# The last attention of a fused two-block transformer kernel: both scores of a query block for two heads issued back to back, then both masks

## What is computed

```python
def dsa_attention(q, k, v, iq, ik, iw, top_k):
    ...
        score = jnp.einsum('bqh,bqhk->bqk', iwb.astype(jnp.float32), jax.nn.relu(dots))
        score = jnp.where(admissible[None], score, -jnp.inf)
        _, sel = lax.top_k(score, top_k)
        kg = jax.vmap(lambda kb, ib: kb[ib])(k, sel)
        vg = jax.vmap(lambda vb, ib: vb[ib])(v, sel)
        valid = (sel // CHUNK) <= qchunk[None, :, None]
        s = jnp.einsum('bqhd,bqkd->bhqk', qb, kg, preferred_element_type=jnp.float32) * scale
        s = jnp.where(valid[:, None], s, -jnp.inf)
        p = jax.nn.softmax(s, axis=-1)
        return jnp.einsum('bhqk,bqkd->bqhd', p.astype(vg.dtype), vg)
```

## Time and profile before

| | |
|---|---|
| median of 3 runs | 2006.15 us (2005.57 to 2012.1) |
| the profiled execution | 2008.66 us, its span 2006.9 us |
| TensorE (PE) busy | 1967.6 us, 98% of the span |
| VectorE (DVE), ScalarE (ACT) busy | 51%, 36% |
| granted TensorE clock, mean | 0.991 of full |
| the last attention | from 1442.4 to about 1546 us |

### The profile page before, as it was taken

One profiled execution on the slowest core, in us unless ns is written; L12 is line 12 of the kernel. 1 busy time (PEld: TensorE's weight loads), 2 busy tenths in 40 slices (PEclk: granted clock), 3 DMA queues, 4 the chain that ended last, 5 costly groups with the idle time before them and its releaser, 6 DMA issues.

```text
span 2006.9 us, 25390 instructions
## 1 busy us (share of the span) xinstructions
PE 1967.6 (98%) x9146; PEld 1585.0 (79%) x9154; DVE 1014.1 (51%) x1572; ACT 719.8 (36%) x1214; POOL 79.1 (4%) x117
## 2 busy tenths in 40 slices
PE   9998999999999999999999999999999999999999
PEld 7776777877888888888888878767777878888887
DVE  6756335656565554633334345767734653333322
ACT  5455434432222222332223234345534433222221
POOL 0001000001111000000000010400000000000000
PEclk9998999999999999899999999999999999999999
DMA  5211122327666554333332323211111223333332
GB/s 173 82 56 63 53 64 73 95 94 231 207 215 210 178 173 147 100 94 94 96 97 89 116 73 95 75 53 43 43 43 43 84 74 116 94 94 103 96 105 94
DMA packets 57521, 207.20 MB, mean 103 GB/s; under 512 B 6449, under 2 KB 6577, under 8 KB 57441
## 3 DMA queue, kind: packets, MB, share of 16 engines
q1 hardware_dynamic: 46800, 167.68, 27.0%
q0 software_dynamic: 10640, 38.44, 6.2%
HBM read 203.96 MB, written 2.10 MB: 103 GB/s over the span
## 4 chain that ended last, share of the span: by engine, by line
PE 89%; DVE 5%; ACT 3%; issue 2%; DMA 1%; SPq 0%; DVEq 0%; ACTq 0%; POOLq 0%
PE PS L437 26%; PE PS L439 25%; PE PS L438 25%; PE PS L862 2%; PE PS L897 2%; PE PS L881 1%; PE PS L667 1%; DMA ADA<-ada 1%; ACT HI L1046 1%; PE PS L559 1%; DVE BIAS L1808 0%; PE PS L590 0%; DMA X<-x_in 0%; PE PS L641 0%; DVE SM L1807 0%
## 5 line engine op out<-in xcount | busy, mean ns | idle before, releaser
L437 PE MATMUL PS<-XH,HI 128*128 128x512 f32 x1552 | 628.9, 405 | 9.8 <-DVE GATE_1M L1876 3.5
L1450 DVE TENSOR_TENSOR LO<-RAW,HI 128x1024 fp32r<-128x1024 f32 x311 | 382.9, 1232 | 456.1 <-ACT HI L1046 455.2
L439 PE MATMUL PS<-XH,LO 128*128 128x512 f32 x1552 | 607.9, 392 | 0.0
L438 PE MATMUL PS<-XL,HI 128*128 128x512 f32 x1552 | 607.2, 391 | 0.0
L1046 ACT ACTIVATE HI<-RAW 128x1024 fp32r<-128x1024 f32 x311 | 328.7, 1058 | 591.9 <-PE PS L439 586.3
L437 PEld LDWEIGHTS PS<-XH,HI 128*128 128x128 f32 x1552 | 293.4, 189 | 88.7 <-issue 26.5
L439 PEld LDWEIGHTS PS<-XH,LO 128*128 128x128 f32 x1552 | 292.7, 189 | 63.1
L438 PEld LDWEIGHTS PS<-XL,HI 128*128 128x128 f32 x1552 | 293.8, 189 | 53.1 <-issue 0.2
L437 PE MATMUL PS<-HIDH,HI 128*128 128x512 f32 x528 | 205.5, 389 | 0.0
L439 PE MATMUL PS<-HIDH,LO 128*128 128x512 f32 x528 | 205.5, 389 | 0.0
L438 PE MATMUL PS<-HIDL,HI 128*128 128x512 f32 x528 | 205.4, 389 | 0.0
(11 more groups left out here) (345 smaller groups left out, 2072.7 us busy)
## 6 DMA issues: line engine op xcount, KB each, us to landing
RAW<-weights SPq DMA_DIRECT2D x311, 512.0 KB, 3.6
ADA<-ada POOLq DMA_DIRECT2D x72, 512.0 KB, 4.6
X<-x_in SPq DMA_DIRECT2D x4, 512.0 KB, 7.1
y_out<-X SPq DMA_DIRECT2D x8, 256.0 KB, 4.6
SQC<-squares SPq DMA_DIRECT2D x1, 320.0 KB, 9.2
TAB_P<-positions POOLq DMA_DIRECT2D x1, 256.0 KB, 4.7
POS<-positions POOLq DMA_DIRECT2D x1, 256.0 KB, 3.3
LAMS<-lambdas POOLq DMA_DIRECT2D x1, 128.0 KB, 5.4
```

Source lines behind the costliest of these rows:

```text
L437: mm(bank, a, moving[0][:, t, :], start=start, stop=False)
L438: mm(bank, a, moving[1][:, t, :], start=False, stop=False)
L439: ins = mm(bank, z, moving[0][:, t, :], start=False, stop=stop)
L1450: V.tensor_tensor(LO[n0 % 3][:], RAW[n0 % 3][:], HI[n0 % 3][:].bitcast(F32), ALU.subtract)\
```

## The change

For attention 3 the units are numbered by pairs of heads: `unit(3, u)` gives head `2 * (u // 8) + u % 2` and block `u % 8 // 2`. So units 0 and 1 are block 0 of heads 0 and 1, units 2 and 3 block 1 of the same heads, and so on. ScalarE and VectorE keep their steps and use the new numbering. TensorE issues scores in even steps alone: both scores, then both masks. The second score now waits, at step `u`, for `probs` of unit `u - 2`, where it waited at step `u + 1` for the same unit. Attentions 1 and 2 stay as they were.

```diff
+        def unit(a, u):
+
+            if a == 3:
+                return 2 * (u // 8) + u % 2, u % 8 // 2
+            return divmod(u, NB)
...
                 for u in range(NU + 3):
-                    if u < NU:
+                    if u < NU and a == 3:
+                        if u % 2 == 0:
+                            for w in (u, u + 1):
+                                h, i = unit(a, w)
+                                n = P * (i + 1)
+                                if w >= 3:
+
+                                    pe.wait_ge(sem("probs"), NU * a + w - 2)
+                                mm(PS[:, w % 3, 0:n], at_["q"](h, i), at_["k"](h, n), start=True, stop=False)
+                            for w in (u, u + 1):
+                                mm(PS[:, w % 3, 0:n], IDENT_B[:], MASK[i][:], start=False, stop=True)\
+                                    .then_inc(sem("scores"), 1)
+                    elif u < NU:
                         h, i = divmod(u, NB)
...
-                        i = v % NB
+                        i = unit(a, v)[1]
...
-                        h, i = divmod(v, NB)
+                        h, i = unit(a, v)
...
-                        n = P * (u % NB + 1)
+                        n = P * (unit(a, u)[1] + 1)
                         act.wait_ge(sem("smax"), NU * a + u + 1)
...
-                        n = P * (u % NB + 1)
+                        n = P * (unit(a, u)[1] + 1)
                         v.wait_ge(sem("scores"), NU * a + u + 1)
```

More of the change, by code:

```diff
@@ L862, in attention @@
                         mm(PS[:, u % 3, 0:n], at_["q"](h, i), at_["k"](h, n), start=True, stop=False)
[L864 to L868, removed]
+                        mm(PS[:, u % 3, n - P:n], IDENT_B[:], CAUSAL_B[:], start=False, stop=True)\
+                            .then_inc(sem("scores"), 1)
                     gate_blocks(u, 0)
@@ L1308, in attention @@
                         v = u - 2
-                        n = P * (v % NB + 1)
+                        n = P * (unit(a, v)[1] + 1)
                         act.wait_ge(sem("pt"), AFTER[a] + v + 1)
@@ L1906, in attention @@
                         w = u - 3
-                        h, i = divmod(w, NB)
+                        h, i = unit(a, w)
                         r = RIN[:, w % 4:w % 4 + 1]
```

## The result

The changed kernel takes 1993.99 us (median of 5 runs, 1992.43 to 1998.57). The kernel before, run again beside it, has a median of 2010.52 us (5 runs, 2005.57 to 2012.1). The ratio is 0.993, with a 95% interval from 0.9917 to 0.9943. By that interval the gain is between 11.5 and 16.7 us. Two later series of the same changed kernel gave ratios of 0.9941 (0.9927 to 0.9956) and 0.9923 (0.9907 to 0.9939). The profiled execution took 1993.99 us where the one before had taken 2008.66.

A forecast was written before the change was run, and what follows sets the result against it. The prediction took TensorE's instructions to bound the kernel. Its terms, 11.6 + 1.6 + 1.3 + 0.3 = 14.8 us, taken off the median of 2006.15 us, gave 1991.4 us, in a range from 1988.5 to 1998.

The forecast's parts named there:

- term 1: Last attention: the second score of each of 16 pairs runs beside the first; 11.6 us saved.
- term 2: Last attention: 16 changes between 64-row and 128-row work vanish, 0.1 us each; 1.6 us, from 0.6 to 1.9.
- The stall at the gate copy: Last attention: TensorE's wait for the gate tile's copy out of bank 7 gets covered; 1.3 us, low end 0.
- The end of the stage: End of the last attention: the 0.4 us wait for the last gate copy shrinks; 0.3 us, ends 0 and 0.4.
- cover that I had claimed: Last attention: the second score's wait for `probs` of unit `u - 2` has 1.5 us or more left at each pair.
- rival with the partial overlap: Last attention: halves overlap only in part, second score costs 0.3 of a single; gain 11.5 us, time 1994.7; chance 3%.
- new wait: Last attention, likeliest at the second score's `probs` wait or a step's transposes: about half the gain lost, 1998.9 us; chance 5%.
- rival in which the second score starts only when the first is through: Last attention: scores of a pair do not overlap, as if a wait held the second; 3.2 us left, 2003.0; chance 4%.
- slower rival: Last attention: exponential of unit `u - 2` late at all 15 pairs; at 1.5 us wait each, 2013.9 us; chance 2%.

The follow-up runs named there:

- first kernel of four scores: Changed kernel with four scores in one visit every fourth step, behind the gate blocks, and value products sharing bank 5; two heads 22.62 us, ratio 0.9946.
- kernel with the later wait: Changed kernel, but the second score of a pair waits for `probs` of unit `u - 1`; stage 96.54 us, ratio 0.9953.
- both heads in the same half: Changed kernel with odd heads reading the even head's partitions 0 to 63; stage 100.52 us, ratio 0.9982.
- two kernels: Changed kernel with both heads' scores in one half of the array, stage 100.52 us; changed kernel with each pair issued twice, stage 100.61 us.
- unpaired kernel: Changed kernel with the differential attention's pair taken apart (score, mask, score, mask); that stage 131.15 us, then 126.48, ratio 0.9974 both times.
- kernel with the mask between: Changed kernel with each score of a last-attention pair followed by its own mask, numbering and steps kept; stage 106.79 us, ratio 1.0011.

## Why the prediction was right, step by step

The forecast was 1991.4 us, in a range from 1988.5 to 1998, and 14.8 us of gain. The time was 1993.99, 2.6 us over. The medians differ by more than forecast, 16.5 us, since the kernel before also rose, from 2006.15 us in three runs to 2010.52 in five. The profiled executions differ by 14.7 us, which is so close in part by chance, as single totals scatter by several microseconds; the stage, which doesn't, differs by 14.3. The mechanism and the sum held, but part of term 1 was put down to the wrong cause, and term 2 was about twice too large.

1. *The second score goes beside the first, 11.6 us.* The size is right (8.5 + 3.2 = 11.7): pairs take the time of singles at every width. But I had put all of it on the two halves. The experiments split it: 8.5 us are columns that run side by side, and 16 x 0.2 = 3.2 us are the fixed cost of a visit, which the second score would no longer pay in the same half either. The rows could have told it: 0.42, 0.63, 0.84 and 1.05 us for 128, 256, 384 and 512 columns are 0.21 for each 128 columns, and 0.21 over.
2. *Changes between 64-row and 128-row work, 1.6 us.* Beside that fixed part there is less left than I took. Two heads became 3.48 us shorter: 2.13 of columns, 2 x 0.19 for the gate wait, and so 0.97 for four visits, 0.24 each, which is also what a 66-row score saves. Less the 0.2 already in term 1 it is 0.04 each, 0.7 us in all, near the low end of 0.6. The low end had the right reading. Entering a score costs 0.12 us more than entering a gate block, in the new profile too (two value products take 0.26 us to the pair and 0.14 to a gate block), and 0.08 of it comes back, since that gate block's first matmul then takes 0.32 us and not 0.23. I had chosen near the high end because of the leaving of 64-row work, and that costs next to nothing: from a 256-column mask to the second matmul of the gate block it is 0.36 us, against 0.11 of mask and 0.23.
3. *The stall at the gate copy, 1.3 us.* It is gone: four transposes take 0.36 us to the gate block. That it is the scores in front of it that cover the wait was shown by the first kernel of four scores, where it came back with 0.3 and 0.6 us.
4. *The end of the stage, 0.3 us.* Four pairs of heads at 3.48 us make 13.9 of the 14.3, which leaves 0.4. The wait for the last gate copy shows it. Before, three transposes took 0.92 us to the next work (1541.58 to 1542.50), 0.42 us of it a named wait; now four take 0.58 (1526.29 to 1526.87), with no wait named.

Of the cover that I had claimed, 1.5 us or more for the second score's wait, the profile shows 2.3. The remark that the odd units are wanted only a pair later was right, and it is needed: at 384 columns the odd unit's exponential ends 0.7 us behind the start of the next pair, and the kernel with the later wait paid for that. The rival with the partial overlap is out (no price of 1.3 singles at any width), and so is the new wait. The rival in which the second score starts only when the first is through was priced too high: 3.2 us were to be left of the gain, but both heads in the same half are that case, and 5.75 us of the stage's 14.3 were left. The slower rival's price, an exponential's lateness at each pair, is nearly confirmed (0.85 us for 0.74), but its condition never arose.

The Trainium skill's page "TensorEngine Tiling (Array Packing)" says under "Key Properties" that changing the tiling mode drains the engine. With that rule the trace agrees, in that a visit costs 0.25 to 0.3 us whatever its width; how much of it is a drain the merged rows don't show. Of the Trainium skill's page "TensorE: Matmul & The Clock Gate", section "Measured speedup vs the span model", the 3.07 for four row tiles does not carry over to two: here a pair cost 1.06 or 1.07 us against 1.05.

## What to carry to other kernels

Take more than one width of an operation from the trace and separate the part that grows with the columns from the part that doesn't; they are removed by different changes. Work on half of the array's rows gains twice when it is grouped: once if the two halves are used by neighbouring instructions, and once for each return to full rows that it saves, even in one half. Before moving such a group, look at which wait it covers where it stands: four scores behind the gate blocks lost 0.6 us for two heads, where the same four in front of them gained 0.5.

## What the runs showed that I had not expected

The 0.2 us in each single score that are not columns, shown above by two kernels, and that 66 rows don't pay most of them. And the clock: it fell to its lower level for short stretches in which TensorE had been busy without a pause. From 110 to 130 us, with 20.00 of 20 us busy, the granted clock was 0.83 and 0.91 in two executions of the unpaired kernel, and it was 0.76 over 7 us in the kernel with the mask between. It was also 0.91 in that stretch, with 20.00 of 20 us busy, in one of three executions of the changed kernel, and 1.00 in the two others. What decides it is open. An expected 131 us came out right in part by that, so a time should be read together with its clock.
